# Summed squares of four norms: one fp32 multiplication with ones, or two fp32r multiplications one tile later

## The reference, cut to what matters

```python
def rmsnorm(x, g):
    xf = x.astype(jnp.float32)
    y = xf * lax.rsqrt(jnp.mean(xf * xf, axis=-1, keepdims=True) + EPS)
    return (y * g.astype(jnp.float32)).astype(x.dtype)

for i in range(DEPTH):                       # DEPTH = 2
    x = x + mixer_i(rmsnorm(x, norm_mix_g[i]))
    x = x + mem_attention(rmsnorm(x, norm_mem_g[i]), rmsnorm(mem, norm_memkv_g[i]), ...)
    x = x + jnp.square(jax.nn.relu(rmsnorm(x, norm_ffn_g[i]) @ w1)) @ w2
return rmsnorm(x, final_norm_g)
```

## Time and profile before

| | us |
|---|---|
| Median of 3 runs | 1173.19 |
| Lowest, highest | 1172.75, 1174.89 |
| The profiled execution | 1173.31 |
| Its span on the core | 1171.4 |
| PE busy with matmuls in the span | 1153.9 (99%) |
| DVE, ACT, POOL busy | 777.8, 518.2, 196.9 |

### The profile page before, as it was taken

One profiled execution on the slowest core, in us unless ns is written; L12 is line 12 of the kernel. 1 busy time (PEld: TensorE's weight loads), 2 busy tenths in 40 slices (PEclk: granted clock), 3 DMA queues, 4 the chain that ended last, 5 costly groups with the idle time before them and its releaser, 6 DMA issues.

```text
span 1171.4 us, 13564 instructions
## 1 busy us (share of the span) xinstructions
PE 1153.9 (99%) x5360; PEld 959.8 (82%) x5360; DVE 777.8 (66%) x890; ACT 518.2 (44%) x687; POOL 196.9 (17%) x147
## 2 busy tenths in 40 slices
PE   8999999999999999999999999999999999999996
PEld 7888888888888888878888888888888888888885
DVE  7787656575585675676488656656767567566577
ACT  7664432453453443545445433433334435344345
POOL 0040044010010010112254053005301001001010
PEclk9999999999999999999999999999999999999999
DMA  9522143465464564435232622215347356556253
GB/s 361 193 90 91 55 165 105 127 143 161 118 152 139 131 164 142 93 86 182 73 109 88 216 89 72 92 37 198 105 112 157 131 126 160 150 121 162 72 95 104
DMA packets 41536, 151.28 MB, mean 129 GB/s; under 512 B 4736, under 2 KB 4864, under 8 KB 40832
## 3 DMA queue, kind: packets, MB, share of 16 engines
q1 hardware_dynamic: 30960, 113.26, 27.6%
q0 software_dynamic: 9216, 33.56, 16.6%
q10 hardware_dynamic: 1296, 3.58, 1.0%
HBM read 148.28 MB, written 2.10 MB: 128 GB/s over the span
## 4 chain that ended last, share of the span: by engine, by line
PE 87%; DVE 7%; DMA 2%; ACT 2%; issue 1%; POOL 1%; SPq 0%; DVEq 0%; ACTq 0%; POOLq 0%
PE psum L1620 21%; PE psum L1622 21%; PE psum L1621 21%; PE psum L1881 7%; PE psum L1882 7%; PE psum L1883 7%; DMA w_raw<-in_weights 1%; DMA w_sum<-in_down 1%; DVE w_lo L1012 1%; DVE y_rows L1293 1%; PE psum L1812 1%; DVE w_lo L1021 1%; POOL sq L1609 0%; DVE b_lo L1036 0%; ACT w_hi L641 0%
## 5 line engine op out<-in xcount | busy, mean ns | idle before, releaser
L1620 PE MATMUL psum<-a_lo,w_hi 128*128 128x512 f32 x704 | 276.1, 392 | 0.0
L1622 PE MATMUL psum<-a_hi,w_lo 128*128 128x512 f32 x704 | 274.0, 389 | 0.0
L1621 PE MATMUL psum<-a_hi,w_hi 128*128 128x512 f32 x704 | 274.0, 389 | 0.0
L1009 DVE TENSOR_TENSOR w_lo<-w_raw,w_hi 128x1024 fp32r<-128x1024 f32 x122 | 154.6, 1270 | 64.9 <-ACT w_hi L628 64.9
L1021 DVE TENSOR_TENSOR w_lo<-w_sum,w_hi 128x1024 fp32r<-128x1024 f32 x112 | 136.0, 1223 | 68.6 <-ACT w_hi L641 68.6
L1881 PE MATMUL psum<-w_lo,s_hi 128*128 128x512 f32 x448 | 174.7, 390 | 3.5 <-DVE y_rows L1293 3.5
L1883 PE MATMUL psum<-w_hi,s_lo 128*128 128x512 f32 x448 | 174.3, 389 | 0.0
L1882 PE MATMUL psum<-w_hi,s_hi 128*128 128x512 f32 x448 | 174.3, 389 | 0.0
L641 ACT ACTIVATE w_hi<-w_sum 128x1024 fp32r<-128x1024 f32 x112 | 117.8, 1056 | 108.5 <-PE psum L1622 52.5
L1620 PEld LDWEIGHTS psum<-a_lo,w_hi 128*128 128x128 f32 x704 | 132.2, 188 | 28.2 <-issue 1.0
L1621 PEld LDWEIGHTS psum<-a_hi,w_hi 128*128 128x128 f32 x704 | 132.2, 188 | 28.1 <-issue 1.0
(11 more groups left out here) (184 smaller groups left out, 1691.7 us busy)
## 6 DMA issues: line engine op xcount, KB each, us to landing
w_raw<-in_weights SPq DMA_DIRECT2D x154, 512.0 KB, 3.6
w_sum<-in_down POOLq DMA_DIRECT2D x64, 512.0 KB, 5.5
w_sum<-in_down SPq DMA_DIRECT2D x48, 512.0 KB, 4.4
x<-in_x_t SPq DMA_DIRECT2D x2, 1024.0 KB, 8.2
x_tok<-in_x_rows SPq DMA_DIRECT2D x2, 1024.0 KB, 7.8
mem_raw<-in_mem_t ACTq DMA_DIRECT2D x1, 1024.0 KB, 4.7
out_rows<-out_rows SPq DMA_DIRECT2D x2, 512.0 KB, 3.3
out_rows<-out_rows SPq DMA_DIRECT2D x4, 256.0 KB, 2.4
```

Of the source, the lines that this page charges most:

```text
L1009: dve.tensor_tensor(w_lo[:, slot, :], w_raw[:, raw, :], w_hi[:, slot, :].bitcast(F32), ALU.subtract).then_inc(wlo_ready, 1)
L1620: pe.matmul(out_ap, s_hi, m_lo, start=start, stop=False)
L1621: pe.matmul(out_ap, s_hi, m_hi, start=False, stop=False)
L1622: return pe.matmul(out_ap, s_lo, m_hi, start=False, stop=stop)
```

## The change

Where the fp32 matmul stood, two fp32r matmuls with an fp32r tile of 1.0 (`ones_r`) now stand: one takes the high part of `ssq`, the other the low part. ACT makes the high part (`hi_squares`), DVE the low part (`lo_squares`), both ahead of the early weight chunks. In attention of layer 1 the totals move from behind query tile 0 to behind tile 1, and two weight chunks are split ahead of the root, as in layer 0. In both MLPs the totals move from behind U0 to behind U1, and the chunks of `hi_ahead` and `lo_ahead` for U0 and U1 are now split ahead of the root. In attention of layer 0 the totals stay where they are. Small tiles are put together in shared 64-byte regions to make room; this moves addresses and adds no instruction. The two other norms of the kernel, which use `sums` and `bcast`, stay as they are. The diff below is cut to what acts:

```diff
+    x2, ssq_lo = at(x2_off, "x2", [P, S]), at(x2_off, "ssq_lo", [P, S], F32R)
+    diag, ssq_hi = at(diag_off, "diag", [P, ST, P]), at(diag_off, "ssq_hi", [P, S], F32R)
+    ones_r = at(region(512), "ones_r", [P, P], F32R)
...
@@ scalar (ACT)
+            def hi_squares(norm):
+                act.wait_ge(ssq_step, SUMMED[norm])
+                act.activation(ssq_hi[:], ssq[:], ACT.Copy).then_inc(ssqhi_ready, 1)
...
-            act.wait_ge(ones_ready, 2)
+            act.wait_ge(ones_ready, 3)
...
             def attention(l, stat):
-                early = 2 - 2 * l
+                early = 2
+                hi_squares(3 * l)
                 for m in range(early):
                     hi_weights(c + m + AHEAD)
                 wide_sd(stat, f"stat_mem_att{l}")
...
+                hi_squares(1 + 3 * l)
+                hi_ahead(l, 0, "U0")
+                hi_ahead(l, 0, "U1")
                 wide_sd(stat, f"stat_ffn{l}")
-                hi_ahead(l, 0, "U0")
                 h_tile(0, 0)
-                hi_ahead(l, 0, "U1")
                 h_tile(0, 1)
                 hi_ahead(l, 0, "U2")
                 h_tile(0, 2)
...
@@ vector (DVE)
+            def lo_squares(norm):
+                n = norm - norm // 3
+                dve.wait_ge(ssqhi_ready, n + 1)
+                dve.tensor_tensor(ssq_lo[:], ssq[:], ssq_hi[:].bitcast(F32), ALU.subtract).then_inc(ssqlo_ready, 1)
...
             dve.memset(ones[:], 1.0).then_inc(ones_ready, 1)
+            dve.memset(ones_r[:].bitcast(F32), 1.0).then_inc(ones_ready, 1)
...
             def attention(l, stat):
-                early = 2 - 2 * l
+                early = 2
+                lo_squares(3 * l)
                 for m in range(early):
                     lo_weights(c + m + AHEAD)
                 wide_root(stat, f"stat_mem_att{l}")
...
+                lo_squares(1 + 3 * l)
+                lo_ahead(l, 0, "U0")
+                lo_ahead(l, 0, "U1")
                 wide_root(stat, f"stat_ffn{l}")
                 relu(0, 0)
-                lo_ahead(l, 0, "U0")
                 relu(0, 1)
-                lo_ahead(l, 0, "U1")
                 lo_ahead(l, 0, "U2")
                 relu(0, 2)
...
@@ tensor (PE)
             def totals(key, norm):
                 wait_bank(key)
-                pe.wait_ge(ssq_step, SUMMED[norm])
-                pe.matmul(bank(key), ones[:], ssq[:], start=True, stop=True).then_inc(sums_ready, 1)
+                pe.wait_ge(ssqlo_ready, norm - norm // 3 + 1)
+                pe.matmul(bank(key), ones_r[:], ssq_hi[:], start=True, stop=False)
+                pe.matmul(bank(key), ones_r[:], ssq_lo[:], start=False, stop=True).then_inc(sums_ready, 1)
...
-            pe.wait_ge(ones_ready, 1)
+            pe.wait_ge(ones_ready, 2)
...
-                    if m == 1 - l:
+                    if m == 1:
                         totals(f"stat_mem_att{l}", norm)
...
                 up(0, 0)
+                up(0, 1)
                 totals(f"stat_ffn{l}", norm)
-                up(0, 1)
                 up(0, 2)
```

More of the change, by code:

```diff
@@ L38 @@
 EPS = 1e-6
+SUMMED = (KT, 3 * KT - 1, 4 * KT - 1, 6 * KT - 2, 8 * KT - 3)
 ATT_SCALE = float(D // HEADS) ** -0.5
@@ L412, in trunk_kernel @@
     ssq = at(region(2 * KB), "ssq", [P, S])
-    x2 = at(region(2 * KB), "x2", [P, S])
-    diag = at(region(2 * KB), "diag", [P, ST, P])
+    x2_off, diag_off = region(2 * KB), region(2 * KB)
+    x2, ssq_lo = at(x2_off, "x2", [P, S]), at(x2_off, "ssq_lo", [P, S], F32R)
+    diag, ssq_hi = at(diag_off, "diag", [P, ST, P]), at(diag_off, "ssq_hi", [P, S], F32R)
+    ones_r = at(region(512), "ones_r", [P, P], F32R)
     ident = at(region(512), "ident", [P, P])
@@ L421, in trunk_kernel @@
     mean_sq = at(region(64), "mean_sq", [P, ST])
-    root_0 = at(region(64), "root_0", [P, ST])
-    root_t = at(region(64), "root_t", [P, ST])
-    sd_mem = at(region(64), "sd_mem", [P, NT])
+    step_off = region(64)
+    root_0, root_t = at(step_off, "root_0", [P, ST]), at(step_off + 32, "root_t", [P, ST])
+    mem_off = region(64)
+    sd_mem, r_mem = at(mem_off, "sd_mem", [P, NT]), at(mem_off + 32, "r_mem", [P, NT])
     first_root = at(region(64), "first_root", [P, 1])
-    r_mem = at(region(64), "r_mem", [P, NT])
-    row_max = at(region(64), "row_max", [P, ST])
-    neg_max = at(region(64), "neg_max", [P, ST])
+    max_off = region(64)
+    row_max, neg_max = at(max_off, "row_max", [P, ST]), at(max_off + 32, "neg_max", [P, ST])
     ssq_tok = at(region(64), "ssq_tok", [P, ST])
@@ L436, in trunk_kernel @@
     half_ssq = at(region(64), "half_ssq", [P, 2, ST])
[L437 to L440, removed]
+    last_off, root_off = region(64), region(64)
+    last_bias, last_ms = at(last_off, "last_bias", [P, ST]), at(last_off + 32, "last_ms", [P, ST])
+    last_sd, last_r = at(root_off, "last_sd", [P, ST]), at(root_off + 32, "last_r", [P, ST])
     assert place[0] <= nc.sbuf_usable_end, (place[0], nc.sbuf_usable_end)
@@ L478, in trunk_kernel @@
     ones_ready = sem("ones_ready")
+    ssqhi_ready = sem("ssqhi_ready")
+    ssqlo_ready = sem("ssqlo_ready")
     max_ready = sem("max_ready")
@@ L1615, in _ @@
         def _(pe):
-            SUMMED = (KT, 3 * KT - 1, 4 * KT - 1, 6 * KT - 2, 8 * KT - 3)
             def three(out_ap, s_hi, s_lo, m_hi, m_lo, start, stop):
```

## The result

The changed kernel takes 1175.89 us (median of 12 runs, 1174.83 to 1177.10) against 1172.95 (12 runs beside them): the ratio is 1.0025, 95% interval 1.0017 to 1.0032. It is 2.9 us slower. The profiled execution is of the faster group.

A forecast was written before the change was run, and what follows sets the result against it. PE, busy in 99% of the span, was taken to bound the kernel. Terms 1.71 (first MLP) + 0.69 (attention 0) + 0.18 (attention 1) - 0.21 (second MLP) = +2.37 us gave 1175.6 against the median; 8-in-10 range 1173.8 to 1177.2.

The forecast's parts named there:

- the sum that I had made from the earlier trace: First MLP: the chain from the totals' end to A11 adds up to 18.06 us.
- I had 1.71: First MLP: PE waits 2.12 us at D0 for A11, making the stretch 1.71 us longer.
- its step of 2.33: First MLP chain: from a relu through ACT's square and high part to DVE's low part of a chunk, 2.33 us.
- (0.69): Attention 0: early chunks queued behind the wait for POOL's sum make the reciprocal late, so the scores come 0.69 us later.
- (0.18): Attention 1: scores' load at 737.11, when PE is ready at 736.84; head 0's transposes end later, net +0.18 us, gain gone.
- (-0.21): Second MLP: the 0.41 us gain less 0.2 for a wait at the banks, net -0.21 us.
- the forecast wait at the copied banks: Second MLP: the second set of transposes waits for the first's banks to be copied out, taken as 0.2 us.
- the reading by which DVE's company behind 84.96 had slowed it: Attention 0: POOL's sum could end as early as 85.23 instead of 86.11, making that term -0.19 us.
- A11 in time: Rival, first MLP: no D0 wait, so that MLP brings -0.41; total 1173.4, or 1172.6 with POOL's early end; chance 0.13.
- wait was passed on behind D0: Rival, first MLP: PE waits again at U6 or D2, one step of 1.14 us more, 1176.7; chance 0.10.
- The fp32r pair did what it says: Rival at the totals: an fp32r product costs half an fp32 one, no PE gain, at most 1.64 more, 1177.3; chance 0.04.
- the line of 0.2%: Whole kernel: about 0.2%, or 2.35 us, is what a measurement can tell from no change; the forecast sum lies on it.

The follow-up runs named there:

- the faster group: Six of the changed kernel's 12 runs, no edit between them: 1174.8 to 1175.2 us, at a mean granted clock of 0.998 or 0.999.
- the reordered kernel: Changed kernel, but in the MLPs ACT makes the high parts of the chunks of D0 and U5 right behind the root: 1172.72 us, ratio 0.9997.
- the other order in attention 0: Changed kernel, but there ACT splits both early chunks ahead of ssq_hi, and DVE makes the first low part ahead of ssq_lo: 1174.99 us, ratio 1.0020.
- the attentions only: Attentions as in the changed kernel, MLPs as before with the fp32 totals: 1173.55 us, ratio 1.0006.
- nine and five products: Changed kernel plus unread PE products between U4 and D0 of the first MLP: nine 1177.37 us, again 1177.55; five 1176.50.
- the slower group: Executions at mean clock 0.995 to 0.997, 1.2 us or more above their kernel's fastest (move alone: by clock); six of the changed kernel's 12, 1176.6 to 1177.1.
- the move alone: Kernel before, with fp32 totals one tile later in both MLPs and the chunks of U0 and U1 split ahead of the root: 1176.90 us, ratio 1.0035.
- the five kernels without a D0 wait over 1 us: Both high parts behind the root 1172.72; only D0's chunk 1173.04; split without move 1173.85; attentions only 1173.55; attentions as before with reordered MLPs 1171.86 and 1172.03.

## Why the prediction was right, and where it was off

**The waits.** The steps of the first MLP came out almost to the hundredth. The chain from the totals' end (203.52 + 0.39 = 203.91) to A11 (220.75 + 1.22 = 221.97) is 18.06 us, the sum that I had made from the earlier trace rows. From the start of U1 to D0's first product the stretch is 1.67 longer (I had 1.71). One reason that I gave is wrong: the chunks of U3 and U4 hadn't filled both waits for ACT. Before, DVE waited 0.51 and 1.65 there; the first grew to 1.65, the second stayed. The sum doesn't suffer, since its step of 2.33 goes from the relu to the low part by way of ACT, whatever DVE does meanwhile. In attention 0 the scores come 0.61 later against the first weights (0.69). What follows the transposes in attention 1 comes 0.14 later (0.18), and the second MLP is 0.28 shorter (-0.21), where the forecast wait at the copied banks showed up as 0.18:

```profile
857.01 0.42 PEld L1919 LDWEIGHTS psum<-ident,x 128*128 128x128 f32 x4 [0.18 <-DVE y_rows L1328]
```

That is 1.67 + 0.61 + 0.14 - 0.28 = +2.14 against +2.37. The faster group of runs, 1175.1, lies 2.2 over before.

**POOL's last add.** I kept its end where it was, against the reading by which DVE's company behind 84.96 had slowed it. It took 2.16 us in the changed kernel too, with DVE's one operation beside its beginning and nothing beside the rest:

```profile
83.18 1.21 DVE L1020 TENSOR_TENSOR w_lo<-w_raw,w_hi 128x1024 fp32r<-128x1024 f32 x1
```

```profile
83.37 2.16 POOL L1588 TENSOR_TENSOR ssq<-ssq,x_sq 128x512 f32<-128x512 f32 x1
```

DVE's operation ends at 84.39 and the add 1.14 behind it. An earlier pair shows the same, with 1.16 from the end of DVE's operation (80.62) to that of the add (81.78), and an add with no such neighbour takes 1.29:

```profile
78.76 1.86 DVE L1020 TENSOR_TENSOR w_lo<-w_raw,w_hi 128x1024 fp32r<-128x1024 f32 x1 [0.65 <-ACT w_hi L632]
```

```profile
78.24 1.29 POOL L1588 TENSOR_TENSOR ssq<-ssq,x_sq 128x512 f32<-128x512 f32 x1 [2.96 <-DVE a_lo L1051]
...
79.68 2.10 POOL L1588 TENSOR_TENSOR ssq<-ssq,x_sq 128x512 f32<-128x512 f32 x1
```

So the add all but stood still until DVE's operation was over. The Trainium skill (SBUF — State Buffer, "Who interferes with whom") says that an operation of DVE with two inputs in SBUF contends with one of GpSimd that reads SBUF, and that this is an exclusive lock. The trace agrees.

**The rivals.** A11 in time didn't happen, but the reordered kernel shows that the slack was there to be had; its 1172.72 lies between the two times given for that rival, 1173.4 and 1172.6. No wait was passed on behind D0: DVE's next relu waits for PE again, at 230.56 by 1.71. The fp32r pair did what it says.

**What was missed.** The median is 0.3 us over the forecast. The measured +0.25% lies over the line of 0.2%, but its interval, 0.17% to 0.32%, takes the line in. The term that was missing is the clock. I priced 2.12 us of standing still as 2.12 us, on a trace whose clock falls nowhere but in the last ten us. The sum of the waits was 0.2 too high, as worked out above. In half of the executions the clock then adds another 1.7, and the median of all runs falls between the two groups: 0.8 over the faster one, and so 0.3 over the forecast. That the median came so near is in part luck: with six executions of twelve in each group it lies in the gap between them, while one group alone would have given 1175.1 or 1176.9. The waits were forecast; the place of the median among the groups was not.

## What to carry to other kernels

When a step is moved behind other work, count two things: the work that it loses as cover, and the waits that already stand in the chain behind it. Here the totals lost one tile of cover, 5.5 us. Moving two weight splits away, 2.3 us of DVE's work, took only 1.2 off the chain, besides 0.9 of waiting for PE, since a wait of 1.65 stayed and another grew from 0.51 to 1.65. What PE then waited was five times the gain in that MLP (2.12 us against 0.41). The cure was to issue the producer's part in its idle time, not to move the step back. Put a new wait behind the work that is ready on that engine, not ahead of it. A new stand-still of PE can cost more than its own length: look at many runs and their clocks, not at one profile.

## What was not expected of the hardware

- In three profiles TensorE's granted clock falls to 0.50, for some 3.4 us: right behind waits of 2.29 and 2.23 us, and in the last half microsecond of one of 2.99. Elsewhere it is 1.00 in the windows of ten us, up to the last ten of the kernel. Behind waits of 2.28 (the changed kernel), 2.28 (the other order in attention 0), 2.13 (the attentions only, at the end of the first MLP), 2.73 and 2.65 (nine and five products) it stayed at 1.00. So in these rows a wait of over 2 us is followed by a fall in some executions and not in others.
- Counting runs: in the slower group were 10 of 20 of the changed kernel, 5 of 12 of the other order in attention 0, 5 of 5 of the move alone, and 8 of 16 of those with products in the gap; but 2 of 66 of the five kernels without a D0 wait over 1 us (one of them run twice), and 3 of 84 of before beside them. Of the 12 of before beside the first result, whose clocks aren't on record, two more lie 2.4 and 3.3 us above the fastest. Taking the wait at D0 away brings the share down from a half to that of the kernel before; this is shown, also where they ran side by side (none of 11 of the reordered kernel beside 4 of 8, 5 of 12 and 5 of 5 of those with the wait). The five kernels without it still have waits elsewhere, the longest of 1.6 to 2.1 us in their profiles. The kernels with products in the gap had no changed kernel beside them. That standing still alone is the cause is supported by the fill products (no fall at D0 in three profiles, and a fall at another wait that had grown) and not settled, since the group itself stayed there.
- What decides between two executions with the same wait, and why the move alone had the lower mean clock every time, is open. So is what makes the adding DMA longer in the three profiles with products in the gap (7.4 to 7.8 us against 6.3 to 6.9).
